# First layer: GpSimd forms one of the two modulation sums, VectorE the other, and the dense weights come in another order

## What is computed

```python
c_act = jax.nn.silu(c)                       # one vector of 1024
for l in range(2):
    mod = c_act @ mod_w[l] + mod_b[l]        # mod_w[l]: 1024 x 6144
    shift1, scale1, gate1, shift2, scale2, gate2 = split(mod, 6)
    h = rms_norm(x, norm1_g[l]) * (1.0 + scale1) + shift1
    mix = diff_fox_mixer(h, ...) if l == 0 else stick_breaking_mixer(h, ...)
    x = x + gate1 * mix
    h = rms_norm(x, norm2_g[l]) * (1.0 + scale2) + shift2
    x = x + gate2 * hier_moe(h, ...)         # 4 groups x 8 experts, 6 MB of weights each
```

## Time and profile before

| | before |
|---|---|
| median of 3 runs | 1255.74 us (1253.07 to 1257.35) |
| the profiled execution: time / span | 1254.81 us / 1252.7 us |
| read from HBM | 488.25 MB, 391 GB/s over the span |
| PE / DVE / ACT / POOL busy | 909.3 / 299.1 / 197.6 / 14.9 us |
| first layer's attention and routing on PE | about 80 to 214 us |
| first layer's experts | 214 to 643 us |

### The profile page before, as it was taken

One profiled execution on the slowest core, in us unless ns is written; L12 is line 12 of the kernel. 1 busy time (PEld: TensorE's weight loads), 2 busy tenths in 40 slices (PEclk: granted clock), 3 DMA queues, 4 the chain that ended last, 5 costly groups with the idle time before them and its releaser, 6 DMA issues.

```text
span 1252.7 us, 13436 instructions
## 1 busy us (share of the span) xinstructions
PE 909.3 (73%) x5515; PEld 419.7 (34%) x5515; DVE 299.1 (24%) x596; ACT 197.6 (16%) x410; POOL 14.9 (1%) x81
## 2 busy tenths in 40 slices
PE   7999999656565556484889999957556565655578
PEld 3445555122221212131348664522121222213133
DVE  1578634001010101010137555501010010101011
ACT  2213414010100100000020454311010101000000
POOL 4000000000000000000000000000000000000000
PEclk9999999788788878777999999988787888877879
DMA  9998897999999999999999936889999999999997
GB/s 357 362 397 280 326 387 279 419 427 427 431 428 427 427 429 429 429 426 428 419 400 408 370 129 268 345 353 428 428 426 428 429 429 429 427 428 426 428 424 303
DMA packets 74605, 489.95 MB, mean 391 GB/s; under 512 B 18092, under 2 KB 18228, under 8 KB 47680
## 3 DMA queue, kind: packets, MB, share of 16 engines
q1 hardware_dynamic: 74256, 488.25, 94.8%
q10 hardware_dynamic: 304, 1.07, 0.3%
HBM read 488.25 MB, written 1.05 MB: 391 GB/s over the span
## 4 chain that ended last, share of the span: by engine, by line
DMA 49%; PE 43%; DVE 3%; SPq 2%; issue 1%; ACT 1%; DVEq 0%; ACTq 0%
DMA tokens<-in_moe_w_dram 46%; PE bank L1128 13%; PE bank L810 8%; PE bank L1161 5%; PE bank L1009 5%; PE bank L863 4%; SPq L510 2%; DMA ring<-in_moe_w_dram 2%; PE bank L738 1%; DMA ring<-in_mod_w_dram 1%; PE bank L931 1%; PE bank L947 1%; PE bank L1095 1%; PE bank L796 1%; PE bank L1172 1%
## 5 line engine op out<-in xcount | busy, mean ns | idle before, releaser
L1128 PE MATMUL bank<-ring,region 128*32 128x512 f32 x1456 | 263.1, 675 | 173.1 <-DMA tokens<-in_moe_w_dram 91.8
L1161 PE MATMUL bank<-ring,region 128*32 128x512 f32 x832 | 143.9, 719 | 131.9 <-DMA ring<-in_moe_w_dram 77.7
L1128 PEld LDWEIGHTS bank<-ring,region 128*32 128x32 f32 x1456 | 69.3, 122 | 351.9 <-issue 288.5
L1128 PE MATMUL bank<-work,region 128*32 128x512 f32 x256 | 134.1, 685 | 0.0
L1128 PE MATMUL bank<-tokens,region 128*32 128x512 f32 x256 | 134.0, 685 | 0.0
L2123 DVE TENSOR_TENSOR region<-region,bank 128x512 f32<-128x512 f32 x16 | 11.0, 688 | 443.6 <-PE bank L1128 443.6
L810 PE MATMUL bank<-ring,tokens 128*128 128x512 f32 x256 | 114.3, 596 | 0.6 <-ACT tokens L1378 0.6
L1161 PEld LDWEIGHTS bank<-ring,region 128*32 128x32 f32 x832 | 37.2, 129 | 224.2 <-issue 189.3
L2133 DVE TENSOR_TENSOR region<-bank,region 128x512 f32<-128x512 f32 x32 | 22.1, 692 | 262.8 <-PE bank L1161 262.8
L1378 ACT ACTIVATE region<-bank,shift,scale 128x128 f32<-128x128 f32 x64 | 24.1, 457 | 358.4 <-PE bank L1115 358.4
L1115 PE MATMUL bank<-region,h 128*128 128x128 f32 x512 | 64.1, 287 | 9.1 <-issue 8.3
(11 more groups left out here) (280 smaller groups left out, 930.0 us busy)
## 6 DMA issues: line engine op xcount, KB each, us to landing
ring<-in_moe_w_dram SPq DMA_DIRECT2D x132, 2048.0 KB, 19.5
work<-in_moe_w_dram SPq DMA_DIRECT2D x22, 2048.0 KB, 24.3
tokens<-in_moe_w_dram SPq DMA_DIRECT2D x22, 2048.0 KB, 28.6
ring<-in_mod_w_dram SPq DMA_DIRECT2D x20, 2048.0 KB, 13.8
ring<-in_moe_w_dram SPq DMA_DIRECT2D x8, 1536.0 KB, 13.5
ring<-in_od_w_in_dram SPq DMA_DIRECT2D x5, 2048.0 KB, 15.0
ring<-in_mod_w_dram SPq DMA_DIRECT2D x8, 1024.0 KB, 14.4
ring<-in_ev_w_in_dram SPq DMA_DIRECT2D x4, 2048.0 KB, 17.7
```

The lines of the kernel that those rows point to most:

```text
L1128: last = pe.matmul(bank[which][32 * j:32 * j + 32, :], m.seated[:, k, 32 * j:32 * j + 32], weights(4 * which + j, k * FE), start=(k == 0), ...
L1161: last = pe.matmul(bank[half][32 * j:32 * j + 32, :], m.hidT[:, c, 32 * j:32 * j + 32], w, start=(c == 0), stop=(c == FC - 1), skip_group_ ...
```

## The change

The DVE now sums the SECOND units (`sum_second`), in the same 16 operations as it summed NEXT before, into `second_sum`; the PE products of SECOND are gone, and one `add_second` (four matmuls with ones) stands in step 8. GpSimd sums the NEXT units, with two operations for what DVE does in one: a multiply in place in the ring slot, then an add to the total, each waiting for the one before. `add_sums` on PE (step 17) now waits for `pool_used` of all four NEXT units. The loads come as SECOND 0, SECOND 1, NEXT 0, SECOND 2, SECOND 3, NEXT 1, 2, 3; the slots are assigned anew. Three half items of the input projection move from steps 5, 6, 7 to steps 6, 8, 9, and the making of the second norm's columns from steps 12, 13 to 9, 10.

```diff
-               [("in", u) for u in range(2, 6)] + [(NEXT, e) for e in range(4)] + [(SECOND, e) for e in range(4)] + GATE_THEN_OUT,
+               [("in", u) for u in range(2, 6)] + [(SECOND, 0), (SECOND, 1), (NEXT, 0), (SECOND, 2), (SECOND, 3),
+                                                    (NEXT, 1), (NEXT, 2), (NEXT, 3)] + GATE_THEN_OUT,
...
-               4: [(10, 0)], 5: [(10, 1)], 6: [(11, 0)], 7: [(11, 1)]},
+               4: [(10, 0)], 6: [(10, 1)], 8: [(11, 0)], 9: [(11, 1)]},
...
-SECOND_PART_AT = (12, 2)
-SECOND_COLS_AT = (13, 4)
+SECOND_PART_AT = (9, 2)
+SECOND_COLS_AT = (10, 4)
...
-NEXT_AHEAD = 4
-NEXT_SUMS = {0: 5, 1: 1, 2: 1, 3: 1, 4: 1, 5: 1, 6: 1, 7: 1}
+SECOND_AHEAD = 4
+SECOND_SUMS = {0: 4, 1: 1, 2: 1, 3: 1, 4: 1, 5: 2, 6: 1, 7: 1}
...
-FIRST_SLOTS = [0, 1, 2, 3, 4, 5, 0, 1, 2, 3, 4, 5, 0, 1, 2, 0, 1, 3, 4, 2, 5, 0, 1, 3]
-FREED = [4, 2, 5, 0, 1, 3]
+FIRST_SLOTS = [0, 1, 2, 3, 4, 5, 0, 1, 2, 3, 4, 5, 0, 1, 2, 0, 1, 3, 2, 0, 4, 1, 3, 2]
+FREED = [5, 0, 4, 1, 3, 2]
...
+    m.second_sum = [m.alone[:, 0:D], m.alone[:, 3 * D:4 * D]]
...
+    pool.wait_ge(m.s["c_act_done"], 1)
+    steps = POOL_STEPS
+    for e in range(MOD_UNITS[NEXT]):
+        slot, count = DENSE_AT[0][MOD_AT[0][NEXT][e]]
+        pool.wait_ge(m.ring_full[slot], 16 * count)
+        for i in range(4):
+            k, w, total = 2 * e + i // 2, slot_rows(m, slot)[:, i // 2, i % 2 * D:(i % 2 + 1) * D], m.cols_sum[i % 2]
+            c = m.c_act[:, k:k + 1]
+            if k:
+                pool.tensor_scalar(w, w, c, None, ALU.mult).then_inc(step, 1)
+                steps += 1
+                pool.wait_ge(step, steps)
+                ins = pool.tensor_tensor(total, total, w, ALU.add)
+            else:
+                ins = pool.tensor_scalar(total, w, c, None, ALU.mult)
...
+                ins.then_inc(m.pool_used, 1)
+                pool.wait_ge(m.pool_used, e + 1)
...
     def add_sums(l):
-        pe.wait_ge(s["cols_summed"], l + 1)
         if l == 0:
+            pe.wait_ge(m.pool_used, MOD_UNITS[NEXT])
             pe.wait_ge(s["sc_moved"], NHH)
+        else:
+            pe.wait_ge(s["cols_summed"], 1)
...
+    def add_second():
+        pe.wait_ge(s["second_summed"], 1)
+        pe.wait_ge(s["proj_copied"], TT * IN_UNITS - 1)
+        for j in range(4):
+            i, half = divmod(j, 2)
+            last = pe.matmul(bank[3][32 * j:32 * j + 32, :], m.ones[:, 0:32], m.second_sum[i][:, half * COL:(half + 1) * COL],
...
-            if l == 0 and SECOND_AT <= step < SECOND_AT + 4:
-                mod_products(l, SECOND, step - SECOND_AT)
+            if l == 0 and step == SECOND_AT:
+                add_second()
```

More of the change, by code:

```diff
@@ L68 @@
 OUT_AT = [[order.index(("out", u)) for u in range(OUT_UNITS)] for order in DENSE_ORDER]
-BY_DVE = [[kind in ((GATE1, SECOND) if l else (NEXT,)) for kind, _ in DENSE_ORDER[l]] for l in range(DEPTH)]
-PE_UNITS = [DENSE_UNITS[l] - sum(BY_DVE[l]) for l in range(DEPTH)]
+BY_DVE = [[kind in ((GATE1, SECOND) if l else (SECOND,)) for kind, _ in DENSE_ORDER[l]] for l in range(DEPTH)]
+BY_POOL = [[l == 0 and kind == NEXT for kind, _ in DENSE_ORDER[l]] for l in range(DEPTH)]
+PE_UNITS = [DENSE_UNITS[l] - sum(BY_DVE[l]) - sum(BY_POOL[l]) for l in range(DEPTH)]
 EARLY_ITEMS = TT * IN_UNITS // 2
 LATE_PARTS = [{0: [(6, 1)], 1: [(7, 0), (7, 1)], 2: [(8, 0), (8, 1)], 3: [(9, 0), (9, 1)],
-               4: [(10, 0)], 5: [(10, 1)], 6: [(11, 0)], 7: [(11, 1)]},
+               4: [(10, 0)], 6: [(10, 1)], 8: [(11, 0)], 9: [(11, 1)]},
               {step: [(6 + step // 2, step % 2)] for step in range(12)}]
@@ L175, in dense_done @@
         return "mod_used", by_dve + (sum(BY_DVE[0]) if l else 0)
-    return "ring_used", l * LAYER_UNITS + u + 1 - by_dve
+    by_pool = sum(BY_POOL[l][:u + 1])
+    if BY_POOL[l][u]:
+        return "pool_used", by_pool
+    return "ring_used", l * LAYER_UNITS + u + 1 - by_dve - by_pool
 def wait_dense(eng, m, l, u):
     name, count = dense_done(l, u)
-    eng.wait_ge(m.mod_used if name == "mod_used" else m.ring_used, count)
+    eng.wait_ge({"mod_used": m.mod_used, "pool_used": m.pool_used, "ring_used": m.ring_used}[name], count)
 def unit_at(i):
@@ L354, in allocate @@
     m.mod_used = sem("mod_used")
+    m.pool_used = sem("pool_used")
     m.got = {n: sem(f"got_{n}") for n in ("x", "c", "small", "mod_cols", "late_cols", "gate_b", "router")}
@@ L625, in program_pool @@
         pool.wait_ge(step, 17)
+    pool.wait_ge(m.s["c_act_done"], 1)
[13 more added lines that the diff above has]
+                ins = pool.tensor_scalar(total, w, c, None, ALU.mult)
+            if i < 3:
+                ins.then_inc(step, 1)
+                steps += 1
+                pool.wait_ge(step, steps)
+            else:
+                ins.then_inc(m.pool_used, 1)
+                pool.wait_ge(m.pool_used, e + 1)
     pool.wait_ge(m.s["sc_moved"], NHH)
     pool.memset(m.carry[:, :], 1.0).then_inc(step, 1)
-    pool.wait_ge(step, 18)
+    pool.wait_ge(step, steps + 1)
     for lo, base in ((0, -1), (P, P - 1), (2 * P, -1)):
         mask(m.carry[:, lo:lo + P], [[-1, P]], 1, ALU.is_gt, 0.0, base=base).then_inc(m.s["carry_ready"], 1)
+POOL_STEPS = 17
 ONES_AND_IDENT = 2
@@ L726, in mod_products @@
         slot = full(l, MOD_AT[l][group][e])
-        if group == SECOND and e == 0:
-            pe.wait_ge(s["proj_copied"], TT * IN_UNITS * (l + 1))
         if group == GATE2 and e == 0 and l == 0:
@@ L773, in add_sums @@
         last.then_inc(s["sums_added"], 1)
+    def add_second():
[4 more added lines that the diff above has]
+            last = pe.matmul(bank[3][32 * j:32 * j + 32, :], m.ones[:, 0:32], m.second_sum[i][:, half * COL:(half + 1) * COL],
+                             start=True, stop=True, skip_group_check=True, tile_position=(0, 32 * j))
+        last.then_inc(s["second_added"], 1)
     def mod_cols(l, group):
@@ L1696, in mod_part @@
             dve.wait_ge(s["sums_added"], 1 + (group == SECOND))
+        elif group == SECOND:
+            dve.wait_ge(s["second_added"], 1)
         else:
@@ L1739, in sum_mods, with sum_second @@
             dve.sem_inc(s["cols_summed"], 1)
-    def sum_next(j, n):
+    def sum_second(j, n):
         for j in range(j, j + n):
             e, i = divmod(j, 4)
-            u = MOD_AT[0][NEXT][e]
+            u = MOD_AT[0][SECOND][e]
             slot, count = DENSE_AT[0][u]
@@ L1907, in attend_even @@
     def attend_even():
-        summed = NEXT_AHEAD
+        summed = SECOND_AHEAD
         for step in range(NHH):
@@ L1922, in attend_even @@
                 norm_heads()
-            sum_next(summed, NEXT_SUMS.get(step, 0))
-            summed += NEXT_SUMS.get(step, 0)
-        dve.sem_inc(s["cols_summed"], 1)
+            sum_second(summed, SECOND_SUMS.get(step, 0))
+            summed += SECOND_SUMS.get(step, 0)
+            if step == max(SECOND_SUMS):
+                dve.sem_inc(s["second_summed"], 1)
         for i in range(2):
@@ L2190, in program_vector @@
             mod_part(0, GATE1)
-            sum_next(0, NEXT_AHEAD)
+            sum_second(0, SECOND_AHEAD)
             attend_even()
```

4 lines of the change are left out of this document (2 added, 2 removed).

## The result

| | before | changed |
|---|---|---|
| median | 1255.7 us (1253.07 to 1257.35) | 1270.27 us (1269.12 to 1271.88, 4 runs) |
| ratio | | 1.0125 (95% interval 1.0108 to 1.0141) |
| the profiled execution: time / span | 1254.81 / 1252.7 us | 1271.88 / 1270.0 us |

The forecast was 1260 us with a range up to 1268: the sign held, the size (+4 against +15) did not.

A forecast was written before the change was run, and what follows sets the result against it. The prediction took PE's start of the experts as the bound. Step 8 +5.3, to step 10 +3.5, then -2.2 and -0.6 gave +6.0 us on the profiled 1254.81, 1260.8, given as 1260 us; range 1251 to 1268 us.

The forecast's parts named there:

- What bounds the kernel: PE's start of the experts, 214.03 us: each microsecond PE comes earlier or later is one of the whole.
- PE's relief of 6.6 us: On PE, four SECOND product units (7.5 us) go and four matmuls with ones (0.9 us) come: net -6.6 us.
- The first rival: DVE and POOL hardly meet: -1.7 us, 1253 to 1255 us, most of PE's saving not had; chance 0.24.
- DVE's own work at nothing: On DVE, the same 16 operations on other weights, with moved column making hidden by a wait: no added time.
- the price of POOL's multiply: Each of 16 multiplies of 128x1024 on POOL taken as 1.17 us, from a fill with selection.
- rival 3: POOL late through adds of 3.1 us, PE stands in `add_sums`, expert loads later: 1264 to 1273 us; chance 0.13.
- the sum of +6.0 us: PE's delay over steps 8 to 14, added step by step: 5.3 + 3.5 - 2.2 - 0.6 us.
- DVE's hold-up, 8.5 us: DVE through step 7: 17 us cannot overlap POOL, half lost by each, so DVE ends at 137.1 us.
- Step 8 to step 10, +3.5: PE between these scores: two products out, two half items and new matmuls in, 11 us against 7.55.
- Steps 10 to 12 and 12 to 14, -2.2 and -0.6: PE between these scores: products removed and `mod_cols` moved, saving 2.2 us, then 0.6 us.
- Both covers: POOL ends about 168 us, 7 us before `add_sums`; the last expert load, landed by 221.5 us, keeps up with PE.
- the rule weighed in the prediction: Shared SBUF ports lock exclusively: a DVE instruction with two SBUF inputs waits for any POOL instruction that reads SBUF.

The follow-up runs named there:

- E1: Not a run: the load of an expert unit, issued by SP; the prediction had it wait for the last NEXT unit, 168 us instead of 145.
- the kernel with the hold-up alone: Changed kernel, but GpSimd runs three units' operations on its own totals only, slots are released once landed, and PE does not wait for it: 1268.22 us, ratio 1.0109.

## Why the forecast was wrong in size and right in sign

- *What bounds the kernel* held: a start of the experts 15.9 us later made 14.6, and in the table the shift of the experts' start and that of the median over its own set's agree within 2.4 us in every kernel, over shifts from -5.6 to +38 us.
- *PE's relief of 6.6 us* held: 5.6 us reach the experts once POOL is silent and the half items stand as before. In the changed order half of it is left (3.1 us). The first rival's remark, that most is not had, was about right for that order.
- *DVE's own work at nothing* nearly held: 1.28 us per sum in the kernel without POOL's sums, where DVE ends step 7 at 129.94 us, 1.3 later than before.
- **The step that failed: the price of POOL's multiply**, "I take 1.17 us", from a fill with selection. It measured 2.84 us. 16 x 1.67 = 27 us more, 20 of them behind 114.8 us: alone POOL would end at 177 us, stretched by DVE it ends at 184 instead of 168 us, and the cover "7 us of room" for `add_sums` and E1 was gone. The range let the add vary up to 3.1 us (rival 3) but gave the multiply no upper end, though the shape had no row for either; with 2.34 us for the multiply as well, rival 3 would have been the forecast. As for that rival: its wait, its place and its effect on the loads came as written, 1270.3 falls in its 1264 to 1273 us, but by the multiply, not by the add.
- **A second step failed beside it: the sum of +6.0 us for the hold-up of DVE and what follows from it.** PE came to `add_sums` 11.8 us late, and the kernel with the hold-up alone, where nobody waits for POOL's results, is 12.5 to 13.5 us slower. Had POOL held DVE as it did and still ended in time, the time would have been some 12 us over before (an estimate from these two), not 4. Its parts are the next two.
- *DVE's hold-up, 8.5 us*: measured 10.8 us against the kernel without POOL's sums (140.69 less 129.94), 12.1 against before. The mechanism is sharper than a shared loss: it is the adds that hold DVE, for what is left of them when DVE comes, and the multiplies hardly do. The scores of step 8: +8.25 instead of +5.3.
- *Step 8 to step 10, +3.5*: measured 15.5 us from one to the other, +8.0. Undisturbed it is 12.0 (so +4.5); the other 3.5 are in the main a wait of 2.32 us for DVE and one half item at the low clock, 5.29 instead of 3.60 us. That PE's clock falls where it stands waiting was in no step of the sum.
- *Steps 10 to 12 and 12 to 14, -2.2 and -0.6*: measured 5.22 and 5.08 us, so -2.24 and -0.61. Exact.
- *Both covers.* With POOL at 184 us both fail at once: `add_sums` waits 2.82 us, and the loads are 13 us short. That is why undoing most of the hold-up, PE's wait, PE's low clock or POOL's late end singly gives 2 us or nothing, and taking away their common source gives 17.

On the rule weighed in the prediction: the traces agree with the Trainium skill (SBUF — State Buffer, "Who interferes with whom") for POOL's adds, which DVE's two-input sums wait out (3.37 instead of 1.28 us), and for fills beside such sums, which don't disturb them (1.28 us). For POOL's tensor_scalar, which reads SBUF too, they agree little: DVE's sums run at 1.28 to 1.30 us over it, or with 0.9 us more (2.16 us for one at 115.17 us in the kernel with the hold-up alone, with such a multiply from 115.22 us on). The figure of the Trainium skill for an add (GPSIMD Engine Reference, section 3.1) is 4497 ns for 2048 elements; half of it, 2.25 us, is an estimate, and the rows here, 2.35 us, bear it out.
